# One token tile runs ahead to its experts; the other two tiles' stages become steps between expert picks

## What is computed

```
h = rmsnorm(x) ;  q_a,k_a,v_a,q_i,k_i,w_i,q_b,k_b,v_b,g_b = split(h @ w_in)
score = sum over 8 index heads of w_i * relu(q_i . k_i) ; keep the top 64 (prompt) or 132 (streams) keys
o_a = softmax(q_a . k_a over the kept keys) @ v_a                        # 8 heads
o_b = silu(g_b) * groupnorm(retention(rotate(q_b), rotate(k_b), v_b))    # 4 heads, carries a state
x = x + concat(o_a, o_b) @ w_out ;  h2 = rmsnorm(x)
for 8 heads:  two products with 128 keys, top 16 of each, top 16 of the 256 sums -> 16 experts
              act = gelu(h2 . u[e]) * gate ;  x = x + act * v[e]         # u, v: 16384 x 1024 each
y = rmsnorm(x)
```

## Time and profile before

| | us |
|---|---|
| median of 3 runs | 1337.76 (1337.74 to 1343.91) |
| the profiled execution | 1342.08 |
| its span, first to last instruction | 1340.3 |
| first gather issued | 279.56 |
| last gather issued | 1314.61 |
| PE / DVE / ACT / POOL busy | 945.8 / 809.5 / 473.8 / 456.4 |

### The profile page before, as it was taken

One profiled execution on the slowest core, in us unless ns is written; L12 is line 12 of the kernel. 1 busy time (PEld: TensorE's weight loads), 2 busy tenths in 40 slices (PEclk: granted clock), 3 DMA queues, 4 the chain that ended last, 5 costly groups with the idle time before them and its releaser, 6 DMA issues.

```text
span 1340.3 us, 11679 instructions
## 1 busy us (share of the span) xinstructions
PE 945.8 (71%) x3478; PEld 414.7 (31%) x3478; DVE 809.5 (60%) x2100; ACT 473.8 (35%) x1448; POOL 456.4 (34%) x424
## 2 busy tenths in 40 slices
PE   6999999976667876666666656766566665665654
PEld 4545544653323222222222212222222221221110
DVE  1044533562786476676776766766667767677544
ACT  2111221142443343343443444424444344443332
POOL 0000001212244245344444445334444443544341
PEclk9858999998889887778888678777887877878787
DMA  9200006469689989999999999999998999999995
GB/s 383 101 12 13 8 1 234 128 228 408 240 335 380 423 324 407 369 421 421 419 396 421 412 419 422 421 371 405 410 421 358 422 420 422 421 420 415 414 422 224
DMA packets 64911, 445.40 MB, mean 332 GB/s; under 512 B 8528, under 2 KB 10192, under 8 KB 13904
## 3 DMA queue, kind: packets, MB, share of 16 engines
q0 software_dynamic: 56800, 407.40, 74.6%
q1 hardware_dynamic: 8048, 37.27, 7.6%
HBM read 438.25 MB, written 3.24 MB: 329 GB/s over the span
## 4 chain that ended last, share of the span: by engine, by line
DMA 40%; PE 36%; DVE 7%; issue 6%; POOL 6%; ACT 4%; SPq 0%; DVEq 0%; POOLq 0%; ACTq 0%
DMA rows<-in_uv,ids 39%; PE ps L438 35%; POOL rows L425 5%; DVE rows L1315 4%; ACT work L831 1%; ACT wgt L831 1%; ACT wt L831 1%; PE ps L441 1%; ACT zact L831 1%; DMA wt<-in_w_q 1%; DMA half<-in_half 0%; DVE rowmax L1063 0%; DVE work L1221 0%; DVE wt L1124 0%; DVE wt L1202 0%
## 5 line engine op out<-in xcount | busy, mean ns | idle before, releaser
L438 PE MATMUL ps<-rows,work 128*64 128x512 f32 x1536 | 495.8, 780 | 345.7 <-ACT work L831 345.0
L425 POOL DMA_INDIRECT rows<-in_uv,ids x384 | 429.9, 1120 | 604.2 <-PE ps L438 524.8
L1315 DVE CUSTOM_DVE_ANT_0 rows<-rows,masks 128x1024 f32<-128x1024 f32 x256 | 313.2, 1227 | 154.0 <-DMA rows<-in_uv,ids 151.0
L438 PEld LDWEIGHTS ps<-rows,work 128*64 128x64 f32 x1536 | 113.4, 165 | 600.3 <-ACT work L831 436.8
L831 ACT ACTIVATE zact<-zdot 128x1 f32<-128x1 f32 x384 | 77.8, 203 | 557.2 <-DVE zdot L1315 551.3
L1315 DVE CUSTOM_DVE_ANT_0 rows<-rows,wt 128x1024 f32<-128x1024 f32 x128 | 157.0, 1226 | 64.6 <-DMA rows<-in_uv,ids 60.9
L831 ACT ACTIVATE work<-pair,wgt 128x64 f32<-128x64 f32 x384 | 133.5, 348 | 12.5
L438 PEld LDWEIGHTS ps<-work,wt 128*128 128x128 f32 x768 | 105.3, 214 | 91.1 <-issue 88.8
L438 PE MATMUL ps<-wt,rows 128*128 128x512 f32 (+4 forms) x326 | 118.1, 509 | 8.7 <-ACT wt L831 5.5
L438 PE MATMUL ps<-work,wt 128*128 128x128 f32 x768 | 122.5, 310 | 1.9 <-DVE work L1213 1.3
L831 ACT ACTIVATE wgt<-zact,gates 128x1 f32<-128x1 f32 x384 | 113.1, 295 | 12.5
(11 more groups left out here) (112 smaller groups left out, 620.4 us busy)
## 6 DMA issues: line engine op xcount, KB each, us to landing
wt<-in_w_q SPq DMA_DIRECT2D x4, 2048.0 KB, 9.1
rows<-in_uv,ids POOLq DMA_INDIRECT x384
wt<-in_w_out SPq DMA_DIRECT2D x2, 2048.0 KB, 18.2
rows<-in_ckv POOLq DMA_DIRECT2D x10, 256.0 KB, 5.5
wt<-in_w_qi SPq DMA_DIRECT2D x1, 2048.0 KB, 14.1
wt<-in_w_qa SPq DMA_DIRECT2D x1, 2048.0 KB, 15.7
wt<-in_w_vb SPq DMA_DIRECT2D x1, 2048.0 KB, 15.9
wt<-in_w_qkb SPq DMA_DIRECT2D x1, 2048.0 KB, 20.4
```

What stands on the lines that cost most here:

```text
L425: pool.indirect_dma_start(row[s], None, a["uv"], bass.IndirectOffsetOnAxis(ap=ids[:, n:n + 1], axis=0)).then_inc(landed[s], 16)
L438: return nc.tensor.matmul(out, lhsT, rhs, start=start, stop=stop)
L1315: V.tensor_tensor_reduce(row[s][:, 0:D], row[s][:, 0:D], h2r[t % 2][:, i % 2, :], 1.0, 0.0, ALU.mult, ALU.add, zdot[:, s:s + 1]).then_inc( ...
```

## The change

The same operations on the same data, in another order and other buffers.

1. **Tile 0 alone.** Norms and the key/value projection are still made for all tiles (the prompt's keys are shared), but everything else is done for tile 0 only: index, attention, retention, output product, queries. Then the first gather is issued. While DVE makes the first two units' choices, PE makes the q_i and q_a products of tiles 1 and 2 (`later_qi`, `later_qa`).
2. **Tiles 1 and 2 as steps.** PE, ACT and DVE each run a loop over the pick number n with a `Clock`; generators (`background` and others) give a step when n has reached its number (`until`). In terms of n: index of tile 1 at 0 to 20, projections v_b, qk_b, g_b of tiles 1 and 2 at 2 to 46, attention of tile 1 at 24 to 46, its retention at 48 to 57, output product at 60 to 75, retention of tile 2 at 80 to 98, its index at 104 to 120, its 17 top-k rounds at 121 to 157, its attention at 160 to 195 (`ATT2` = 160, a step every 4 picks), its output product at 196 to 207. The loop of PE has even n only.
3. **Weights stream.** The four query weights share one slot and are loaded for each tile again: 10 loads of 2 MB instead of 4 (`Q_LOADS`; the last of a tile serves as the first of the next). w_out is loaded twice, and so are parts of x and three tables.
4. **Smaller things.** ids and gates are a ring of 4 units; q, score and spread results each have one PSUM place instead of two; some of POOL's small steps (`take_rstd`, `group_rstd`, memsets) stand between gathers.

The core of the diff:

```diff
+        class Clock:
+            now = -1
+            def until(self, n):
+                while self.now < n:
+                    yield
+            def tick(self, n, *gens):
+                self.now = n
+                for gen in gens:
+                    next(gen, None)
...
+            def load_q(k):
+                if k > 0:
+                    sp.wait_ge(q_ps, [u for u in range(UNITS) if q_load(u) < k][-1] + 1)
+                sp.dma_start(wt[:, 0, :], a[f"w_q{Q_LOADS[k]}"]).then_inc(w_in["q"], 16)
...
             def gather(n):
...
+                if n == 4:
+                    pool.wait_ge(qi_ps, 3)
+                if n == 6:
+                    pool.wait_ge(qa_ps, 3)
                 if n >= G:
                     pool.wait_ge(acc, (n - G) // 2 + 1)
...
# PE
+                yield from until(ATT2)
+                scores_2(0)
+                yield
+                for b in range(STREAMS):
+                    yield
+                    prob_t2(b)
+                    if b + 1 < STREAMS:
+                        scores_2(b + 1)
+                    yield
+                    values_2(b)
...
+            gens = (next_spreads(), background(), next_queries(), projections())
+            for n in range(0, UNITS * KP, 2):
+                if n % (HP * KP) == 0:
+                    y_start(n // (HP * KP))
+                add_experts(n, n % (HP * KP) == HP * KP - 2)
+                clock.tick(n, *gens)
...
# ACT
+                for b in range(STREAMS):
+                    yield from until(ATT2 + 5 + 4 * b)
+                    prob_t2(b)
+                    yield
+                    if b + 1 < STREAMS:
+                        exp_2(b + 1)
+                    yield
+                    values_2(b)
...
+            for n in range(UNITS * KP):
+                t = n // (HP * KP)
+                weigh(n)
+                clock.tick(n, *gens)
...
# DVE
+                for b in range(STREAMS):
+                    yield from until(ATT2 + 1 + 4 * b)
+                    row_max(ATT[2] + b, psf[:, 0:640].rearrange("p (j n) -> p j n", j=1), 1)
+                    yield from until(ATT2 + 3 + 4 * b)
+                    scale_probs(ATT[2] + b, prob2[:, b % 2:b % 2 + 1, :], 1)
```

More of the change, by code:

```diff
@@ L183, in build @@
-        ckv = [at(wtf, 4 * SLOT + b % 7 * 1024, 1024) if b in (0, 1, 7) else
-               at(rowf, 12288 + (b - 2) * 1024, 1024) if b < 5 else at(rowf, (b - 5) * 1024, 1024)
[L185 to L191, removed]
-        rot = at(work, 2688, TILES * 512).rearrange("p (t h e d) -> p t h e d", t=TILES, h=2 * HB, e=2)
+        PLACE = (4, 5, 6, 7, 0, 1, 2, 3)
@@ new lines, in _, with next_queries @@
+            later_qi(3)
+            query(1)
+            query_scores(1)
+            spread_out(0)
+            later_qa(0)
+            later_qa(1)
+            spread_out(1)
+            later_qa(2)
+            later_qa(3)
+            clock = Clock()
+            until = clock.until
+            def next_queries():
+                for u in range(2, UNITS):
+                    yield from until(q_at(u))
+                    for part in range(8):
+                        query_part(u, part)
+                        if part % (4 if u < 4 else 2) == 1:
+                            yield
+                    yield from until(scores_at(u))
+                    query_scores(u)
@@ new lines, in _ @@
+            act.wait_ge(vb_ps, 1)
+            copy(vb0, ps[:, 7, :]).then_inc(vb_sb, 1)
+            act.wait_ge(smax, 1)
+            for j in range(8):
+                ins = A(prob0[:, j, :], ps[:, j // 4, j % 4 * P:(j % 4 + 1) * P], ACT.Exp,
+                        bias=negmax[:, j:j + 1], scale=DH ** -0.5, accum_out=esum[:, j:j + 1])
+            ins.then_inc(expd, 1)
+            act.wait_ge(gb_ps, 1)
+            A(gs0, ps[:, 7, :], ACT.Silu).then_inc(gb_sb, 1)
+            act.wait_ge(rt_ps, 1)
@@ new lines, in exps_1, with prob_t1 @@
+            def exps_1(c):
+                act.wait_ge(smax, ATT[1] + c + 1)
+                if c == 1:
+                    act.wait_ge(pt_ps, PT[1] + 2)
+                for j in range(4):
+                    ins = A(prob1[:, j, :], ps[:, j // 2, j % 2 * 256:(j % 2 + 1) * 256], ACT.Exp,
+                            bias=negmax[:, j:j + 1], scale=DH ** -0.5, accum_out=esum[:, j:j + 1])
+                ins.then_inc(expd, 1)
+            def prob_t1(c, half):
+                act.wait_ge(pt_ps, PT[1] + 2 * c + half + 1)
+                if c == 1 and half == 0:
+                    act.wait_ge(pv_ps, 2)
+                copy(probT1[:, half, :, :], bank4(2)).then_inc(pt_sb, 1)
@@ new lines, in _, with next_top16 @@
+            mean_square(H2_STAT[0])
+            normed(h2, H2_STAT[0], 0, g2b, hready)
+            h2_take(0)
+            whole(top16(0))
+            spread_take(0)
+            whole(top16(1))
+            spread_take(1)
+            clock = Clock()
+            until = clock.until
+            def next_top16():
+                for u in range(2, UNITS):
+                    start = scores_at(u) + 1
+                    yield from until(start)
+                    for i, _ in enumerate(top16(u)):
+                        if u not in (2, 16) or i % 2:
+                            yield
```

1851 lines of the change are left out of this document (1048 added, 803 removed).

## The result

The changed kernel takes **1513.62 us** (median of 4 runs, 1509.53 to 1521.41), the kernel before beside it 1337.75 (1332.57 to 1343.91): ratio **1.132**, 95% interval 1.1253 to 1.1386. It is 176 us slower. The forecast was 1362, the range 1265 to 1425: the sign was right, the size was not. The profiled execution takes 1514.11, its span is 1512.3.

A forecast was written before the change was run, and what follows sets the result against it. It took the DMA engines to bound the kernel from about 400 us. Head 147, picks 0 to 216 762, remaining gathers 405, weight loads 15 and tail 26 made 1355; with 10 for the clock, 1362 on the median's scale, range 1265 to 1425.

The forecast's parts named there:

- Head: Start of the kernel, tile 0 alone: first gather at about 128 us, 151 earlier; first pair added at about 147.
- the clock's 10: PE in the waiting stages: a tenth more on some 100 us of work, +10 us, bounds 0 and 45.
- stage sum: Picks 0 to 216, stage by stage at full clock: 762 us, 3.5 per pick, against 610 on the queue.
- Extra bytes: Queue during the picks: 36.5 MB of other transfers, 87 us at 421 GB/s, part of the floor of 1198.
- Coupling as the mechanism: Steps between picks: a product read one pick later ties pairs into a chain slower than the queue's 4.98 us per pair.
- the signs named: First pair by 150 us, DMA share 0.75 to 0.85, Exps 17 to 20 us apart, relus 7, longer DVE waits for PE.
- rival (b): PE at half clock in the waiting stages: 1390 to 1430 instead of 1362; counted within the forecast's 0.57.
- Per-pair price 5.9: A coupled pair costs 5.9 us (1.94 on PE plus 4.0) plus PE work ahead of the product and DVE's item.
- Table rule: Trainium skill's 1.38 us drain per ScalarE table switch: 33 us more, sum 1387; set aside for the row's 1.28 per load.
- rival (a): Queue stays fed, only closed chains cost: 1275, or some 1305 with half the other excesses; range 1260 to 1330, chance 0.34.
- Rival (c): Gain and loss cancel: 1331 to 1344, needing 730 to 743 us for picks 0 to 216; chance 0.09.
- Rival (d): Query weights come late through one slot: 10 us for each of 9 loads, +90; one chance in twenty.

The follow-up runs named there:

- e9: e5 without the six repeated query weight loads (12.6 MB): 1246.7 us, ratio 0.933 to the kernel before.
- e1: Changed kernel with tile 2's attention regrouped, two streams every 8 picks, products read later: 1450.2 us, ratio 1.089 to the kernel before.
- e2: Changed kernel with DVE's start of a unit's choices three picks behind the score product instead of one, gates' Exp two later: 1473.3 us, ratio 1.106.
- e8: Changed kernel with ACT's copy of a unit's query two picks later and DVE's copy of ids and gates one later: 1476.9 us, ratio 1.108.
- e7: Changed kernel with the moves of e1, e2 and e8 together: 1365.6 us, ratio 1.028 to the kernel before.
- e5: Changed kernel with nearly every PE product read at n+3 instead of n+1, same products and bytes: 1268.2 us, ratio 0.954 to the kernel before.
- e12: e5 with one wait added: in picks 256 to 375 DVE waits after every second dot for PE's pair: 1448.4 us, ratio 1.089 to the kernel before.
- e4: Changed kernel with background Exps and Silus replaced by a Relu of the same size, 23 table loads fewer: 1490.7 us, ratio 1.118.
- e13: e12 with four added products of zeros per pair in PE's waits, picks 256 to 376: 1413.7 us, ratio 1.061 to the kernel before.
- e6: Changed kernel with four added products of zeros after each pair in picks 0 to 216: 1531.4 us, ratio 1.154 to the kernel before.
- e10: e5 with background Exps and Silus replaced by a Relu of the same size, 16 table loads fewer: 1256.6 us, ratio 0.940.
- e3: Changed kernel without the six repeated query weight loads (12.6 MB): 1502.1 us, ratio 1.127 to the kernel before.

## Why the prediction was wrong in size and right in kind

- **Head**: nearly right. First gather 132.75 (forecast 128), but the first pair starts at 153.7 and is added, by the gather that waits for it, at 156.6: 9.6 us after the forecast's 147 and later than its sign, 150. The difference of the span, 1512.3 against 1355 before the clock's 10, is these 9.6, 146.4 of stage sum and 1.3 of the rest.
- **Extra bytes**: right, and hidden where the steps are; before pick 216 they cost only when the reads were moved (e9).
- **Coupling as the mechanism**: right. It is the cause: moving reads takes the time out, place by place and additively (e1, e2, e8, e7), all together turn the change into a gain (e5), and one added wait puts it back (e12). Of the rivals, bytes are worth 1 us of stage sum and tables at most 24; the 8, 4 and 7 table loads that e1, e2 and e5 also lose are a small part of their gains. PE's clock rose with the moved reads, from 0.78 to 0.86 over picks 0 to 216 in e5, but PE's busy time fell only from 565 to 498 us there, so the clock is at most some 68 of the 245 us. Of the signs named, the DMA share (0.74 from 156 to 1065 us) and DVE's waits came out so, while the distances were longer: Exps 24.0 us apart instead of 17 to 20, relus 9.2 instead of 7.
- **The stage sum, 762, is the step that failed**, by 146 us, in two of its terms. First the **clock**. The prediction had both levels and even the half-clock length of an attention step, 23.8 us, where 23.5 was measured (in part luck: the stage was granted 0.73, and moving the starts of the choices alone took it to 192.6); but the forecast took full clock and a tenth of 100 us, +10, with 45 as the bound. The pairs of picks 0 to 216 in the changed kernel, and in the same picks of the kernel before (309 to 908 us):

```profile
L502 PE MATMUL ps<-rows,work 128*64 128x512 f32 x866 | 306.7, 846 | 337.7 <-ACT work L1027 337.7
```
```profile
L438 PE MATMUL ps<-rows,work 128*64 128x512 f32 x864 | 276.1, 772 | 189.5 <-ACT work L831 189.1
```

  The first group (157 to 1065 us) is 108 pairs in 306.7 us, 97 more than at 1.94 each. For picks 64 to 216, to which the bound of 45 belongs, it is 72 more (76 pairs in 219.6 us), for the pairs alone. The price was to be had from the trace before: there a pair took 2.56 us in these picks, at 0.81. The argument "the queries keep coming between the steps" did not hold, and the row read for rival (b), 0.52 in the index stage, does not show a waiting PE: in it PE is busy for 43.74 of 44 us. Rival (b), 1390 to 1430, named this and still stopped short. Second, **couplings that I left out or thought hidden**: the start of the choices and the copies of query and ids, in nearly every unit. Moving them was worth 81 us of stage sum (43.8 + 37.6), against a few single items in my stage sums. The two terms overlap, since a freed pair also runs at a higher clock, so they can't be added up to 146.
- **Per-pair price 5.9**: 8.26 measured, 1.6 of the difference clock and some 0.6 a second choice step that the pair in the earlier trace rows did not have.
- **Table rule weighed and left**: right (e4).
- **Sums**: the links of the attention step add up to 17.1, not 17.2, those of the index step to 7.1, not 7.3; in rival (a) the index and the top-k rounds are 17 and 11 over the queue's, not 15 and 9, and 1275 + 34 is 1309. None of this moves the total by more than 5 us.
- **Rival (a), "the queue stays fed", 1275**: wrong for this kernel. That e5 takes 1268 does not bear it out: there the couplings are taken away and not hidden. e5's span, 1266.1, is 68 us over the floor of 1198. **Rival (c)** needed a stage sum of 730 to 743.
- **Rival (d), late weights**: no wait of PE for a query weight is among the changed kernel's larger waits, and six loads less gave 6 to 12 us.
- **Rest after pick 216**: 446 forecast, 447 measured.

What stays open: how the 146 us split between clock and extra couplings inside each stage, since filling PE's waits there disturbed as much as it gave. It is not shown either how much of e1's gain is the grouping and how much the later readers.

## What to carry over

When stages are threaded between the iterations of a loop whose engines work in order, don't ask whether an item is small, but when its reader comes: read at n + 1, it ties the next iteration's whole chain to the product; with nearly all items read at n + 3, the change went from 13% slower to 5% faster here. One coupling in a while is hidden while the transfers set the pace; couplings that follow each other are not. Count every such reader, the loop's own (queries, choices, copies) too, and price PE's work on such a chain at what it took in a trace with waits (a pair 3.52 us in e12), not at full clock (1.94). Two small items in one step with later readers took less time here than one item in every second step (143.3 against 205.6 us).

## What the runs showed of the hardware

- In a run of coupled pairs PE was granted 0.62 to 0.67 of its clock while it was busy for half of the time (e12, windows of 100 us), against 0.79 in the same stretch uncoupled (e5), where it was busy for 189 of 303 us; products of zeros in the waits lifted it to 0.81 to 0.85 (e13). The clock was not what limited everywhere: 0.98 instead of 0.85 in picks 0 to 16 changed nothing (e6).
- A table load of ScalarE took 1.28 us. What leaving one out gave depended on the place: 1.06 us each in the coupled attention (17.0 for 16, e4), 1.1 in picks 16 to 48 of the kernel with later reads (9.1 for 8, e10) and 0.5 in its attention (4.0 for 8).
- The same 12.6 MB of loads cost 6 to 12 us in the coupled kernel (e3) and 21 to 28 in the one with later reads (e9).
